# Expert passes with twelve resident up slabs instead of eight, and PE's up loop as three turns of twelve and eight behind them

## The chip, the cores and the metric

The kernel runs as one program on one core of a Trainium2 chip. The metric is the device time of one execution in microseconds. All data are float32. TensorE (PE) is fed by weight loads (PEld) that run beside its matmuls; VectorE (DVE) and ScalarE (ACT) empty the accumulators; SyncE (SP) issues all transfers from HBM, in program order, on one queue.

## What is computed

One step of a two-layer decoder for 288 tokens: 256 of a prompt and 8 sequences of 4 tokens. Each layer mixes tokens by three recurrent branches and then runs a SwiGLU. In layer 0 that is one dense SwiGLU, in layer 1 it is a mixture of eight experts, and only this last part is touched here:

```python
def swiglu(h, w1, w3, w2):
    return (jax.nn.silu(h @ w1) * (h @ w3)) @ w2

def moe_swiglu(h, router, w1, w3, w2):
    logits = (h @ router).astype(jnp.float32)
    top_v, top_i = lax.top_k(logits, TOP_K)          # TOP_K = 2 of 8
    probs = jax.nn.softmax(top_v, axis=-1)
    gate = jnp.sum(jax.nn.one_hot(top_i, N_EXPERTS, dtype=jnp.float32) * probs[..., None], axis=-2)
    out = jnp.zeros(h.shape, jnp.float32)
    for e in range(N_EXPERTS):
        out = out + gate[..., e:e + 1] * swiglu(h, w1[e], w3[e], w2[e]).astype(jnp.float32)
    return out.astype(h.dtype)
```

The model width is 1024 (KT = 8 tiles of 128), the hidden width 2816 (FT = 22 tiles of 128).

## The kernel before

**Passes.** The experts are worked off one after the other, one pass for each. A pass gathers the tokens of its expert into at most 88 columns (the four experts with the most tokens, `LARGE`) or 76 columns (the other three of the `FIXED` seven passes, and all `rest` passes behind them). In this profile there are eight passes: four of 88 columns, then four of 76, the last of which is the one turn of the `rest` loop.

**Slabs.** Weights come in slabs. An up slab is 128 x 1024 values, 512 KB, and gives one hidden tile of `h @ w1` (even numbers) or `h @ w3` (odd numbers); a pass has `UP_SLABS` = 44. A down slab belongs to `h @ w2`; a pass has 24, of which every third is 384 KB and the others 512 KB. For each slab PE makes 8 products, each as two halves of 64 rows (`narrow_products`, L447), so 16 matmuls. In float32 one matmul of the code is two MATMUL and two LDWEIGHTS records in the profile: 704 matmuls of an up part are 1408 records of each kind.

**Where slabs lie.** Up slab n lies in slot n % 8 of `ring` (`RING` = 8). Down slab d lies in slot d % 6 of `down_ring`, which is a part of `proj`. A semaphore for each slot (`slab_in`, `down_in`) tells PE that a slab has landed; one counter, `slab_done`, tells SP how many slabs PE has used up.

**PE's pass** (`expert`, L2679): a hardware loop `Fori` of five turns over eight up slabs (L2683), four up slabs behind it, the transposes of the scatter matrix (L2646), the gathering of the next pass's tokens (`gather_tokens`, L2617 and L2624), and a loop of four turns for the down part: two times three down slabs (L2659), two scattering products (L2670) and two transposes (L2677). The pass itself is the body of a hardware loop, and this body stands in PE's program three times: for the four large passes (L2717), for the three smaller ones (L2719), and for `rest` (L2722).

**SP's order in a pass** (L2526 to L2541, L2541 to L2555 for `rest`), which is what sets the order of the transfers: down slabs 0 to 5; up slabs 8 to 43; the first eight up slabs of the following expert, in the order `FREED` = 4, 5, 6, 7, 0, 1, 2, 3, each into the slot whose last slab of this pass is used up; down slabs 6 to 23. Each waits for its slot, and all behind it wait with it. The last pass too loads eight slabs of a following expert, though none follows. Up slab n waits until slab n - 8 is used up, down slab d until slab d - 6 is.

**Ahead of the passes.** While PE joins the branches of layer 1 (the pairs q of `join_slabs`; q below `BRANCH0` = 3 are the gates), SP loads the last two groups of `w_mix` slabs into the ring and then up slabs 0 to 7 of the first expert. `y_ret` (128 x 8 x 288) holds sums for the gates' products, `lora_w` (128 x 8 x 272) the weight sums of the first pair; neither is used after q = 2.

Of the kernel before, what the change touches and what calls it, by code (L numbers as in the profile page):

```python
# [22 lines left out]
D = 1024  # L23
# [7 lines left out]
KT = D // 128  # L31
# [7 lines left out]
FT = FF // 128  # L39
NE = 8  # L40
CAP, LAST_CAP, LARGE = 88, 76, 4
FIXED = NE - 1
# [8 lines left out]
RING = 8  # L51
# [34 lines left out]


UP_SLABS = 2 * FT
DOWN_SLABS = 24
HALF = T // 2  # L90
PAIRS_UP, PAIRS_DOWN = KT // 2, FT // 2
# [127 lines left out]
def build(nc, xT_in, w_mix, w_lora, w_rank, w_gkup, vec_in, vecf_in, router_in, w_ff, s_ret, s_gla, s_rw,  # L219
# [130 lines left out]
            self.end = w.at  # L350

    slab_in = [nc.alloc_semaphore(name=f"slab_in{s}") for s in range(RING)]
    slab_done = nc.alloc_semaphore(name="slab_done")
    rank_in = [nc.alloc_semaphore(name=f"rank_in{s}") for s in range(2)]
    wr = lora_w[:, :, :].rearrange("p k n -> p (k n)")[:, 0:512].rearrange("p (s n) -> p s n", s=2)
# [77 lines left out]
    def slab_arrived(pe, p, g, s):  # L433
        pe.wait_ge(slab_in[s], (g + (fills_before(layer, s) + fills(p, s) + 1)) * 16)

    def load_ff_slab(sp, e, j, s, done, n=KT):

        sp.wait_ge(slab_done, done)
        sp.dma_start(ring[:, s, 0:n], w_ff[e, j, :, 0:n]).then_inc(slab_in[s], 16)
# [5 lines left out]
            mm = nc.tensor.matmul(out, ring[:, s, k, :], x, start=(k0 + k == 0), stop=(k0 + k == last - 1))  # L445
        mm.then_inc(slab_done, 1)

    def narrow_products(pe, s, out, rhs, n=KT, k0=0, last=KT):

        for k in range(n):  # L450
            for c in range(2):
                mm = nc.tensor.matmul(out[64 * c:64 * c + 64], ring[:, s, k, 64 * c:64 * c + 64], rhs[:, k0 + k, :],  # L452
                                      start=(k0 + k == 0), stop=(k0 + k == last - 1))
        mm.then_inc(slab_done, 1)

    FIRST, MIDDLE, LAST_TWO = bank[0:6:3], bank[1:6:3], bank[2:6:3]
# [1665 lines left out]
    def mix_out(nc, block, sig, layer, delta, joined):  # L2122
# [31 lines left out]
        @block.sync  # L2154
        def _(sp):
            load_group(sp, S_RW_OUT, 1)
            load_first_group(sp, S_OUT)
            if dense:
                for j in range(FF_SLABS):
                    load_ff_slab(sp, 0, j, j % RING, FF0 + j - RING + 1, dense_slab_width(j))  # L2160
                    if j == UP_SLABS:
                        sp.wait_ge(sig("normed"), KT)
                        sp.dma_start(vec[:, :], vec_in[layer + 1]).then_inc(sig("next_vec"), 16)
                        sp.dma_start(lora_w[:, :, :], w_lora[layer + 1]).then_inc(sig("next_low"), 16)
                        sp.dma_start(gkup[:, :], w_gkup[layer + 1]).then_inc(sig("next_up"), 16)
                load_next_layer(sp)
                sp.wait_ge(sig("next_up"), 16)
            else:
                for j in range(RING):
                    load_ff_slab(sp, 1, j, j, FF0 + j - RING + 1)  # L2170
# [287 lines left out]
    def experts(nc, block, sig, layer, merge, rs):  # L2458
# [28 lines left out]
        HG, SC, DOWN, SUM = bank[4:8], bank[1], bank[2:4], bank[0]  # L2487
        OTOK, ADD = (bank[6], bank[4]), (bank[7], bank[5])
        FF0 = slabs_before(layer, len(STREAM))
        FREED = 4, 5, 6, 7, 0, 1, 2, 3  # L2490
        TILES = ((0, 128), (128, 128), (256, 32))

        def passes(eng):
# [12 lines left out]
        @block.sync  # L2506
        def _(sp):
            def freed_up(p, n):

                if n >= RING:  # L2510
                    return count(p, FF_SLABS, FF0 + n - RING + 1)
                return count(p, FF_SLABS, FF0 - FF_SLABS + max(range(n, UP_SLABS, RING)) + 1)

            def load_up(p, e, n):
                load_ff_slab(sp, e, n, n % RING, freed_up(p, n))

            def load_down(p, e, d):
                if d >= DRING:
                    sp.wait_ge(slab_done, count(p, FF_SLABS, FF0 + UP_SLABS + d - DRING + 1))
                else:  # L2520
                    sp.wait_ge(slab_done, count(p, FF_SLABS, FF0 - DRING + d + 1))
                n = slab_width(UP_SLABS + d)
                sp.dma_start(down_ring[:, d % DRING, 0:n], w_ff[e, UP_SLABS + d, :, 0:n]).then_inc(down_in[d % DRING], 16)

            e = 1
            for q in range(FIXED):  # L2526
                p = 0, q
                for d in range(DRING):
                    load_down(p, e, d)
                for n in range(RING, UP_SLABS):  # L2530
                    load_up(p, e, n)
                if q == 0:
                    sp.wait_ge(sig("ctl"), 1)
                following = sp.value_load(ctl[0:1, q:q + 1], min_val=1, max_val=NE)
                for n in FREED:
                    load_up((0, q + 1), following, n)
                for d in range(DRING, DOWN_SLABS):
                    load_down(p, e, d)
                e = following
            rest = passes(sp)  # L2540
            with sp.Fori(0, rest) as i:  # L2541
                e = sp.value_load(ctl[0:1, bass.ds(i + (FIXED - 1), 1)], min_val=1, max_val=NE)
                following = sp.value_load(ctl[0:1, bass.ds(i + FIXED, 1)], min_val=1, max_val=NE)
                p = i, FIXED
                for d in range(DRING):
                    load_down(p, e, d)
                for n in range(RING, UP_SLABS):
                    load_up(p, e, n)
                for n in FREED:
                    sp.wait_ge(slab_done, freed_up((i, FIXED + 1), n))  # L2550
                    settle(sp)
                    sp.dma_start(ring[:, n], w_ff[following, n]).then_inc(slab_in[n], 16)
                for d in range(DRING, DOWN_SLABS):
                    load_down(p, e, d)
            for k in range(0, KT, 2):  # L2555
                sp.wait_ge(sig("normed"), k + 2)
                sp.dma_start(yT_out[:, k:k + 2, :], hT[:, k:k + 2, :]).then_inc(sig("stored"), 16)
            sp.wait_ge(sig("stored"), 4 * 16)
            for s in range(RING):
                per = len(range(s, UP_SLABS, RING))  # L2560
                fill = fills_before(layer, s) + fills(len(STREAM), s) + FIXED * per + 1
                sp.wait_ge(slab_in[s], rest * (per * 16) + fill * 16)
                settle(sp)

        @block.tensor
        def _(pe):
# [62 lines left out]
            def up(p, cap, n, turn):  # L2629

                i, done = p
                s = n % RING
                per = len(range(s, UP_SLABS, RING))
                fill = fills_before(layer, s) + fills(len(STREAM), s) + done * per + n // RING + 1
                pe.wait_ge(slab_in[s], turn * 16 + (i * (per * 16) + fill * 16))
                pe.wait_ge(sig("w3_free" if n % 2 else "w1_free"), turn * (RING // 2) + count(p, FT, n // 2 + 1))
                if n in (2, 3):
                    pe.wait_ge(sig("oT"), count(p, KT, n - 1))
                narrow_products(pe, s, bank[n % 4][:, 0:cap], hg[:, :, 0:cap])

            def scatter_matrix(p):

# [36 lines left out]
            def expert(p, cap, next_cap):  # L2679

                pe.wait_ge(sig("hg"), count(p, 1, 1))
                settle(pe)
                with pe.Fori(0, UP_SLABS // RING) as g:  # L2683
                    for n in range(RING):
                        up(p, cap, n, g)
                for n in range(UP_SLABS // RING * RING, UP_SLABS):
                    up(p, cap, n, 0)
                scatter_matrix(p)
                pe.wait_ge(sig("otok"), count(p, KT, 2))
# [621 lines left out]
```

## Time and profile before

| | us |
|---|---|
| median of 3 runs | 2503.94 |
| lowest and highest | 2503.2, 2506.28 |
| the profiled execution, whole | 2506.55 |
| its span, first to last instruction | 2504.8 |
| outside the span | 1.75 |
| stretch of the eight expert passes in the span | 1772.0 to 2490.4 |

A row of the timeline shows instructions of one line of the code that follow each other without a wait; the time in brackets is how long the engine was idle before them, and what ended that. "issue" stands for a wait that nothing in the profile explains: no semaphore, no transfer of data. In the rows of the windows the share of the DMA engines goes slightly over 1 where packets overlap. Queue q1 carries the data, q8 and q14 carry instructions to the engines.

### The profile page before, as it was taken

Reading aid. Unit: us, or ns where it says so; the run is one execution under the profiler, and the core shown is the slowest. Engines: PE = TensorE matmul, PEld = TensorE weight load, DVE = VectorE, ACT = ScalarE, POOL = GpSimd, SP = SyncE. Lnnn points to the kernel's source line nnn. Section 1 sums busy time; section 2 is a strip of 40 time slices with the busy share of each in tenths; the row PEclk is TensorE's granted clock in tenths of the full one; section 3 lists DMA queues with packets and bytes.
Section 4 is the critical chain, followed back from the end, with each engine's and each line's share of the span. In section 5 each row is a group of like instructions: output and inputs, shape, how many; then the busy total and the mean of one; then the engine's idle time right before and its main releaser. Section 6 shows DMA issues by size and latency. Waiting matters only on the chain. (4 is left out here: it accounts for less than half of the span.)

```text
span 2504.8 us, 103575 instructions
## 1 busy us (share of the span) xinstructions
PE 2448.9 (98%) x45930; PEld 2047.9 (82%) x45930; DVE 1288.9 (51%) x3327; ACT 609.0 (24%) x1798; POOL 0.2 (0%) x4
## 2 busy tenths in 40 slices
PE   9999999999999999999999999999999999999998
PEld 8987666666698999898766666679899999888986
DVE  7666666666686676756665666667311111111111
ACT  2233333433311100223333334321111111111111
POOL 0000000000000000000000000000000000000000
PEclk9999999999999999999999999999999999999999
DMA  6334432222243444333443222234899999999997
GB/s 249 111 136 162 150 134 88 83 83 79 90 163 121 159 173 134 133 116 137 154 161 125 84 77 83 83 105 152 321 357 391 385 364 386 393 388 397 407 391 284
DMA packets 146066, 500.42 MB, mean 200 GB/s; under 512 B 18785, under 2 KB 23521, under 8 KB 143361
## 3 DMA queue, kind: packets, MB, share of 16 engines
q1 hardware_dynamic: 145792, 496.44, 54.3%
q8 instruction: 213, 3.49, 0.6%
q14 instruction: 61, 0.49, 0.1%
HBM read 476.08 MB, written 20.29 MB: 198 GB/s over the span
## 5 line engine op out<-in xcount | busy, mean ns | idle before, releaser
L299 PE MATMUL psum<-hT,ring 128*64 128x144 f32 (+1 forms) x4568 | 457.1, 345 | 3.8 <-DVE hT L2419 1.7
L452 PE MATMUL psum<-work,ring 128*64 128x88 f32 (+1 forms) x11264 | 423.8, 235 | 10.3 <-issue 4.3
L452 PEld LDWEIGHTS psum<-work,ring 128*64 128x64 f32 x11264 | 411.6, 136 | 23.4 <-issue 20.5
L299 PEld LDWEIGHTS psum<-hT,ring 128*64 128x64 f32 x4568 | 291.7, 137 | 97.6 <-issue 12.2
L2959 DVE TENSOR_TENSOR work<-psum,work 128x88 f32<-128x88 f32 x176 | 43.9, 249 | 363.5 <-PE psum L452 363.3
L2659 PE MATMUL psum<-work,proj 128*64 128x88 f32 (+1 forms) x5632 | 212.1, 234 | 4.1 <-issue 2.7
L2659 PEld LDWEIGHTS psum<-work,proj 128*64 128x64 f32 x5632 | 205.1, 136 | 10.8 <-issue 9.6
L1765 ACT ACTIVATE work<-psum 128x256 f32<-128x256 f32 (+4 forms) x320 | 104.0, 362 | 349.7 <-PE psum L1676 84.8
L299 PE MATMUL psum<-y_ret,work 128*64 128x144 f32 x2400 | 157.9, 288 | 0.8 <-DVE y_ret L529 0.8
L299 PE MATMUL psum<-work 128*64 128x144 f32 (+4 forms) x2096 | 154.1, 282 | 4.3 <-DVE work L1256 3.6
L299 PEld LDWEIGHTS psum<-y_ret,work 128*64 128x64 f32 x2400 | 150.3, 138 | 1.2 <-issue 1.2
L299 PEld LDWEIGHTS psum<-work 128*64 128x64 f32 (+2 forms) x2096 | 121.3, 136 | 30.7 <-issue 11.3
L2950 DVE TENSOR_TENSOR xT<-xT,psum 128x288 f32<-128x288 f32 x64 | 29.1, 454 | 224.9 <-PE psum L2670 223.9
L2744 ACT ACTIVATE work<-psum 128x88 f32<-128x88 f32 x176 | 43.0, 244 | 376.5 <-PE psum L452 376.3
L299 PE MATMUL psum<-y_ret,ring 128*64 128x144 f32 (+1 forms) x1280 | 126.8, 332 | 2.5 <-ACT work L1765 2.5
L299 PEld LDWEIGHTS psum<-y_ret,ring 128*64 128x64 f32 x1280 | 79.5, 137 | 18.4 <-ACT work L1765 4.5
L321 PE MATMUL psum<-hT,ring 128*128 128x288 f32 x252 | 72.8, 408 | 0.0
L1561 PEld LDWEIGHTS psum<-work 64*64 64x64 f32 x1408 | 47.3, 134 | 29.4 <-issue 17.7
L544 DVE TENSOR_TENSOR y_gla<-psum,y_gla 128x288 f32<-128x288 f32 x72 | 32.9, 458 | 73.3 <-PE psum L299 72.7
L2748 ACT ACTIVATE work<-psum 128x88 f32<-128x88 f32 x64 | 15.7, 245 | 222.8 <-PE psum L2659 222.8
L299 PE MATMUL psum<-hT,work 128*64 128x144 f32 x928 | 68.8, 287 | 0.0
L516 DVE TENSOR_TENSOR work<-ring 128x512 f32<-128x512 f32 (+1 forms) x90 | 54.6, 607 | 19.1 <-PE psum L299 19.1
(514 smaller groups left out, 3725.9 us busy)
## 6 DMA issues: line engine op xcount, KB each, us to landing
ring<-w_ff_dram SPq DMA_DIRECT2D x424, 512.0 KB, 6.9
ring<-w_mix_dram SPq DMA_DIRECT2D x256, 512.0 KB, 4.4
proj<-w_ff_dram SPq DMA_DIRECT2D x128, 512.0 KB, 5.5
proj<-w_ff_dram SPq DMA_DIRECT2D x64, 384.0 KB, 5.7
work<-s_gla_dram SPq DMA_DIRECT2D x8, 1024.0 KB, 5.4
gla_s_out<-work SPq DMA_DIRECT2D x8, 1024.0 KB, 4.7
work<-s_ret_dram SPq DMA_DIRECT2D x8, 512.0 KB, 5.6
ret_s_out<-work SPq DMA_DIRECT2D x8, 512.0 KB, 3.0
```

Of the source, the lines that this page charges most:

```text
L299: last = nc.tensor.matmul(out[64 * c:64 * c + 64], weights[:, 64 * c:64 * c + 64], x, start=start, stop=stop)
L321: mm = (in_halves if self.narrow else nc.tensor.matmul)(out, ring[:, s, k, :], rhs[:, k, :], start=(k == 0), stop=(k == KT - 1))
L452: mm = nc.tensor.matmul(out[64 * c:64 * c + 64], ring[:, s, k, 64 * c:64 * c + 64], rhs[:, k0 + k, :], start=(k0 + k == 0), stop=(k0 + k = ...
L516: op.tensor_tensor(s1, a21, a22, ALU.add).then_inc(sig("wsum"), 1)
L544: nc.vector.tensor_tensor(c[:, 1:3, :], two(LAST_TWO[side]), c[:, 5:7, :], ALU.add).then_inc(sig("outer"), 1)
L1561: last = mm(unit(half(W, r), c), half(AT, 1 - r)[:, c], half(X, 1 - r)[:, c], start=True, stop=True)
L1765: return nc.scalar.activation(out, in_, func, **kw)
L2659: last = mm(DOWN[m][64 * h:64 * h + 64, 0:cap], down_ring[:, d, k, 64 * h:64 * h + 64], hid[:, KT * c + k, 0:cap], start=(KT * c + k == 0) ...
L2744: ac(act1[:, f % 2, :], bank[2 * f % 4][:, 0:CAP], ACT.Silu).then_inc(sig("w1_free"), 1)
L2748: ac(oT[:, m % 2, :], DOWN[m % 2][:, 0:CAP], cp).then_inc(sig("oT"), 1)
L2950: tt(xT[:, k, :], xT[:, k, :], ADD[m % 2][:, 0:T], ALU.add).then_inc(sig("added"), 1)
L2959: tt(hid[:, f, :], bank[(2 * f + 1) % 4][:, 0:CAP], act1[:, f % 2, :], ALU.mult).then_inc(sig("w3_free"), 1)
```

## The change

- The up slabs get a ring of twelve slots, `UP_RING` = 12: the eight of `ring`, two in `y_ret` and two in `lora_w`, with a semaphore each (`extra_in`). Up slab n lies in slot n % 12. `down_ring` stays at six.
- PE's up loop has three turns of twelve slabs, and eight slabs stand behind it, in each of the three copies of the pass.
- SP loads up slabs 8 to 11 of the first expert while the branches are joined, as soon as the slabs of pair q = 2 are used up. In a pass it loads down slabs 0 to 5, up slabs 12 to 43, then twelve up slabs of the following expert, `FREED` = 8, 9, 10, 11, 0, ..., 7, then down slabs 6 to 23. Up slab n waits until slab n - 12 is used up.
- `narrow_products` is written with `in_halves`; the matmuls are the same, and the profile names them by another line (L300 of the changed file in place of L452).

```diff
+UP_RING = 12
...
+    extra_in = [nc.alloc_semaphore(name=f"extra_in{s}") for s in range(UP_RING - RING)]
+    up_in = slab_in + extra_in
...
+    extra_slots = [x.rearrange("p k n -> p (k n)")[:, D * j:D * j + D].rearrange("p (k n) -> p k n", k=KT)
+                   for x in (y_ret[:, :, :], lora_w[:, :, :]) for j in range(2)]
+    up_slots = [ring[:, s] for s in range(RING)] + extra_slots
...
             load_group(sp, S_RW_OUT, 1)
+            if not dense:
+                sp.wait_ge(slab_done, join_done(BRANCH0 - 1))
+                for n in range(RING, UP_RING):
+                    sp.dma_start(up_slots[n], w_ff[1, n]).then_inc(up_in[n], 16)
             load_first_group(sp, S_OUT)
...
-        FREED = 4, 5, 6, 7, 0, 1, 2, 3
+        FREED = 8, 9, 10, 11, 0, 1, 2, 3, 4, 5, 6, 7
...
-                if n >= RING:
-                    return count(p, FF_SLABS, FF0 + n - RING + 1)
-                return count(p, FF_SLABS, FF0 - FF_SLABS + max(range(n, UP_SLABS, RING)) + 1)
+                if n >= UP_RING:
+                    return count(p, FF_SLABS, FF0 + n - UP_RING + 1)
+                return count(p, FF_SLABS, FF0 - FF_SLABS + max(range(n, UP_SLABS, UP_RING)) + 1)
...
-                for n in range(RING, UP_SLABS):
+                for n in range(UP_RING, UP_SLABS):
                     load_up(p, e, n)
...
-                with pe.Fori(0, UP_SLABS // RING) as g:
-                    for n in range(RING):
+                with pe.Fori(0, UP_SLABS // UP_RING) as g:
+                    for n in range(UP_RING):
                         up(p, cap, n, g)
-                for n in range(UP_SLABS // RING * RING, UP_SLABS):
+                for n in range(UP_SLABS // UP_RING * UP_RING, UP_SLABS):
                     up(p, cap, n, 0)
```

PE's program in the first copy of the pass, before: the end of the loop's turn (slabs 6 and 7), the loop's branch, the four slabs behind it and the scatter transposes.

```order
L2635 ISA
L2636 ISA
L452 MATMUL psum<-work,ring 64x88 x32
L2683 REGISTER_ALU
L2683 COMPARE_AND_BRANCH
L2635 ISA
L2636 ISA
L452 MATMUL psum<-work,ring 64x88 x32
L2636 REGISTER_ALU
L452 MATMUL psum<-work,ring 64x88 x32
L2644 REGISTER_ALU
L2646 MATMUL psum<-table,work 88x128 x2
```

The same place now, from slabs 8 and 9 of the turn (in `y_ret`) on.

```order
L300 MATMUL psum<-work,y_ret 64x88 x32
L2649 ISA
L300 MATMUL psum<-work,lora_w 64x88 x32
L2696 REGISTER_ALU
L2696 COMPARE_AND_BRANCH
L2648 ISA
L2649 ISA
L300 MATMUL psum<-work,ring 64x88 x32
L2649 REGISTER_ALU
L300 MATMUL psum<-work,ring 64x88 x32
L2648 REGISTER_ALU
L2649 REGISTER_ALU
```

The loop's body grew from 128 to 192 matmuls and the part behind it from 64 to 128, so a copy of the pass has 128 matmuls more.

SP's program around the transfers for the following expert, first pass, before: the end of the up slabs, the reading of the expert's number, the first two of the eight.

```order
L439 DMA ring<-w_ff_dram 128x1024 x36
L2534 TENSOR_LOAD ctl
L2534 ISA x2
L439 ISA
L439 DMA ring<-w_ff_dram 128x1024
```

The same place now, with the first four of the twelve and the fifth.

```order
L2529 DMA ring<-w_ff_dram 128x1024 x8
L2548 TENSOR_LOAD ctl
L2548 ISA x2
L2529 ISA
L2529 DMA y_ret<-w_ff_dram 128x1024
L2529 ISA
L2529 DMA y_ret<-w_ff_dram 128x1024
L2529 ISA
L2529 DMA lora_w<-w_ff_dram 128x1024
L2529 ISA
L2529 DMA lora_w<-w_ff_dram 128x1024
```

Between the last up slab of a pass and its down slab 6 there stand twelve transfers now, eight before; ahead of them in the pass there are 32 up slabs to load instead of 36.

## Rows read from the trace of the kernel before

**Rows 1.** The page: span, engines, the queues of section 3.

```profile
span 2504.8 us, 103575 instructions
...
PE 2448.9 (98%) x45930; PEld 2047.9 (82%) x45930; DVE 1288.9 (51%) x3327; ACT 609.0 (24%) x1798; POOL 0.2 (0%) x4
...
q8 instruction: 213, 3.49, 0.6%
```

**Rows 2.** The chain that ended last, the passes: start us, us, what.

```profile
1864.59 54.50 PE psum L452 x1408
1919.09 0.51 PE psum L2646 x3
...
1955.88 54.54 PE psum L452 x1408
...
2226.38 10.93 PE psum L452 x320
```

**Rows 3.** The timeline of PEld, sixth pass: start us, us, what, [idle before <-releaser].

```profile
2226.37 18.28 PEld L452 LDWEIGHTS psum<-work,ring 128*64 128x64 f32 x544 [0.58 <-issue]
2244.94 1.12 PEld L452 LDWEIGHTS psum<-work,ring 128*64 128x64 f32 x32 [0.28 <-DMA ring<-w_ff_dram]
2246.43 2.28 PEld L452 LDWEIGHTS psum<-work,ring 128*64 128x64 f32 x64 [0.37 <-issue]
...
2279.43 0.17 PEld L2646 LDWEIGHTS psum<-table,work 128*88 128x88 f32 x2
...
2289.92 3.01 PEld L2659 LDWEIGHTS psum<-work,proj 128*64 128x64 f32 x88 [0.19 <-DMA proj<-w_ff_dram]
2293.34 3.14 PEld L2659 LDWEIGHTS psum<-work,proj 128*64 128x64 f32 x88 [0.40 <-issue]
...
2313.31 19.46 PEld L452 LDWEIGHTS psum<-work,ring 128*64 128x64 f32 x576 [0.55 <-issue]
```

**Rows 4.** Windows, whole core: one large pass, then ten-us pieces of the sixth.

```profile
1864.00:1955.00 91.00, 90.70 (x2235) 87.12 (x2234) 13.29 (x41) 11.95 (x41) 0.00 (x0) 1.00 0.99 379
...
2250.00:2260.00 10.00, 9.52 (x256) 8.78 (x253) 1.00 (x4) 0.98 (x4) 0.00 (x0) 1.00 1.03 410
...
2290.00:2300.00 10.00, 9.72 (x250) 8.70 (x252) 1.04 (x3) 1.34 (x7) 0.00 (x0) 1.00 1.03 407
2300.00:2310.00 10.00, 9.85 (x260) 8.84 (x256) 0.91 (x2) 1.17 (x5) 0.00 (x0) 1.00 0.97 363
2310.00:2320.00 10.00, 9.71 (x264) 8.81 (x262) 1.41 (x4) 2.70 (x7) 0.00 (x0) 1.00 0.99 363
```

**Rows 5.** DMA of 1900 to 2100, queues: packets, MB, share of 16 engines.

```profile
q1 hardware_dynamic: 21531, 76.30, 99.9%
q14 instruction: 4, 0.03, 0.1%
```

**Rows 6.** DMA of 1866 to 1867, and of 2145 to 2146.

```profile
q8 instruction: 1, 0.02, 5.8%
...
q8 instruction: 1, 0.02, 6.3%
```

**Rows 7.** The timeline of PEld, first time through the second copy (pass five).

```profile
2138.28 8.12 PEld L452 LDWEIGHTS psum<-work,ring 128*64 128x64 f32 x243 [0.49 <-issue]
2147.54 0.53 PEld L452 LDWEIGHTS psum<-work,ring 128*64 128x64 f32 x13 [1.14 <-issue]
...
2194.84 0.86 PEld L2659 LDWEIGHTS psum<-work,proj 128*64 128x64 f32 x24
2196.54 4.29 PEld L2659 LDWEIGHTS psum<-work,proj 128*64 128x64 f32 x127 [0.83 <-issue]
2201.25 0.86 PEld L2659 LDWEIGHTS psum<-work,proj 128*64 128x64 f32 x24 [0.42 <-issue]
```

**Rows 8.** The timeline of SP while the branches are joined, before the passes.

```profile
1703.18 21.38 SPq L420 DMA_DIRECT2D ring<-w_mix_dram  x8
1732.92 22.85 SPq L439 DMA_DIRECT2D ring<-w_ff_dram  x8
```

More of the change, by code:

```diff
@@ L434, in slab_arrived, with up_fills @@
         pe.wait_ge(slab_in[s], (g + (fills_before(layer, s) + fills(p, s) + 1)) * 16)
+    extra_slots = [x.rearrange("p k n -> p (k n)")[:, D * j:D * j + D].rearrange("p (k n) -> p k n", k=KT)
+                   for x in (y_ret[:, :, :], lora_w[:, :, :]) for j in range(2)]
+    up_slots = [ring[:, s] for s in range(RING)] + extra_slots
+    def up_fills(s):
+        return fills_before(layer, s) + fills(len(STREAM), s) if s < RING else 0
     def load_ff_slab(sp, e, j, s, done, n=KT):
@@ L446, in slab_products, with narrow_products @@
         mm.then_inc(slab_done, 1)
[L448 to L453, printed above, removed]
+    def narrow_products(out, slab, rhs):
+        for k in range(KT):
+            mm = in_halves(out, slab[:, k, :], rhs[:, k, :], k == 0, k == KT - 1)
         mm.then_inc(slab_done, 1)
@@ L2508, in freed_up @@
             def freed_up(p, n):
-                if n >= RING:
-                    return count(p, FF_SLABS, FF0 + n - RING + 1)
-                return count(p, FF_SLABS, FF0 - FF_SLABS + max(range(n, UP_SLABS, RING)) + 1)
+                if n >= UP_RING:
+                    return count(p, FF_SLABS, FF0 + n - UP_RING + 1)
+                return count(p, FF_SLABS, FF0 - FF_SLABS + max(range(n, UP_SLABS, UP_RING)) + 1)
             def load_up(p, e, n):
-                load_ff_slab(sp, e, n, n % RING, freed_up(p, n))
+                sp.wait_ge(slab_done, freed_up(p, n))
+                sp.dma_start(up_slots[n % UP_RING], w_ff[e, n]).then_inc(up_in[n % UP_RING], 16)
             def load_down(p, e, d):
@@ L2546, in _ @@
                     load_down(p, e, d)
-                for n in range(RING, UP_SLABS):
+                for n in range(UP_RING, UP_SLABS):
                     load_up(p, e, n)
@@ L2551, in _ @@
                     settle(sp)
-                    sp.dma_start(ring[:, n], w_ff[following, n]).then_inc(slab_in[n], 16)
+                    sp.dma_start(up_slots[n], w_ff[following, n]).then_inc(up_in[n], 16)
                 for d in range(DRING, DOWN_SLABS):
@@ L2558, in _ @@
             sp.wait_ge(sig("stored"), 4 * 16)
[L2559 to L2562, printed above, removed]
+            for s in range(UP_RING):
+                per = len(range(s, UP_SLABS, UP_RING))
+                sp.wait_ge(up_in[s], rest * (per * 16) + (up_fills(s) + FIXED * per + 1) * 16)
                 settle(sp)
@@ L2631, in up @@
                 i, done = p
[L2632 to L2636, printed above, removed]
+                s = n % UP_RING
+                per = len(range(s, UP_SLABS, UP_RING))
+                fill = up_fills(s) + done * per + n // UP_RING + 1
+                pe.wait_ge(up_in[s], turn * 16 + (i * (per * 16) + fill * 16))
+                pe.wait_ge(sig("w3_free" if n % 2 else "w1_free"), turn * (UP_RING // 2) + count(p, FT, n // 2 + 1))
                 if n in (2, 3):
                     pe.wait_ge(sig("oT"), count(p, KT, n - 1))
-                narrow_products(pe, s, bank[n % 4][:, 0:cap], hg[:, :, 0:cap])
+                narrow_products(bank[n % 4][:, 0:cap], up_slots[s], hg[:, :, 0:cap])
             def scatter_matrix(p):
```

## The prediction

> **What bounds the kernel now.** I read the page first: PE is busy for 98% of a span of 2504.8 us [rows 1]. That says that PE is nearly always occupied, not that it is the limit, so next come the chain that ended last and PE's timeline for the expert passes, the only part that the change touches in earnest. They show two regimes.
>
> In a pass of 88 columns the up part is one piece of 1408 records in 54.5 us without a wait [rows 2], 1.24 us a slab. One pass after the other takes 91.3 us (1864.59 to 1955.88). Here PE is the limit.
>
> In a pass of 76 columns PE needs 1.09 us a slab (320 records, ten slabs, in 10.93 us [rows 2]). It keeps that up for 17 slabs, then waits for a transfer, and from there on stops before every pair of slabs for 0.2 to 0.4 us [rows 3]: 13 pairs from 2246.43 to 2279.43, 2.54 us a pair, where PE alone would need 2.19. In that stretch the DMA engines move 410 GB/s [rows 4], which is 1.28 us for 512 KB, 2.56 for a pair. So the small passes go at the speed of the transfers. Were no slab late, the up part would take 44 x 1.09 = 48.0 us instead of 53.1 (2226.37 to 2279.43): 5.1 us of waiting in each of four passes, 20 us in all. That is what the twelve slots are aimed at.
>
> **The change part by part.**
>
> *Slabs 8 to 11 of the first expert, loaded early.* Four more transfers of 512 KB, 5.1 us of DMA time, are queued at q = 2. The next transfers behind them on SP's queue start at 1703.18 in this profile and the last eight end at 1755.8 [rows 8], eight transfers spread over 21 us in each group because they wait for slots, so the four fit between. Cost 0; without the cover at most 5.
>
> *Twelve slots in the up part.* A pass moves 60 slabs of 512 KB and 8 of 384 KB, 34.6 MB, before and after: 84.4 us at 410 GB/s, against 86.9 us for the sixth pass (2226.37 to 2313.31 [rows 3]). Nothing is taken away, so a ring can gain only what the DMA engines do not use: 2.5 us there. The question is where PE waits instead. SP's queue is in order, so I count what stands in it ahead of down slab 6 at the start of a pass: before, the last four or so of down slabs 0 to 5, 36 up slabs, 8 of the following expert, and slab 6 itself, 49 transfers; now 4 + 32 + 12 + 1 = 49. Down slab 6 is the 49th either way and lands at the same moment. Before, PE starts it at 2289.92 after a short wait for its transfer, and waits again 3.4 us later [rows 3]: it comes just in time, 10.5 us behind the end of the up part. Now PE ends the up part 5.1 us earlier and waits about 5 us more for down slab 6. Saved 4 x 5.1, paid back 4 x 5.1. The same holds in the last pass, where twelve slabs that nobody uses, not eight, stand ahead of it.
>
> What is left is the 2.5 us a pass of unused transfer time. It lies where PE uses down slabs slowly and SP waits for slots: 407 GB/s until 2300, then 363 [rows 4]. Those waits are on down slabs 12 to 23 and on the first up slab of the next pass, which have the slots they had. So 0, with a gain of 4 x 2.5 = 10 us as the bound and 2 us of loss as the other. In the large passes the DMA engines move 379 GB/s on average [rows 4] and nothing is late now: 0.
>
> *PE's program.* This is the part that I think decides. Of its 44 slabs a copy of the pass writes out 20 instead of 12. A matmul of the code is four instructions for the engine, as the records show (1408 MATMUL and as many LDWEIGHTS for 704). Counted through the program, a copy has 329 matmuls and 44 other instructions, 1360 in all; now 457 and 55, 1883. The whole program of PE has 55,232, and q8 brought 213 packets of 16.4 KB [rows 1]: one packet is about 256 instructions, and each part of the program came once. The trace confirms the size. On the first way through the second copy PE stops with "issue", and two such stops lie 127 weight loads and as many matmuls apart, 254 instructions [rows 7]: it stops where a new packet begins. From the first of them (243 weight loads in) the second copy begins some 15 instructions behind a border, and the first copy, 5.3 packets earlier, three quarters into a packet.
>
> So before, the first copy touches seven packets, the last by a few instructions. As PE enters that one, at the end of the first pass of this copy, another is brought ahead: the packet at 1866 [rows 6]. Eight, then, and from 1900 to 2100, over two further jumps back to the start of the copy, q8 brings nothing at all [rows 5]. The engine holds at least eight packets, and the trace shows no code of more than eight that runs twice. Now the first copy is 7.4 packets from three quarters into one: it touches nine, with one ahead ten. The second touches eight, with one ahead nine. If the store is the round eight that the trace shows full, the packet that the jump back needs has been overwritten each time.
>
> The Trainium skill, "Runtime: NRT & Kernel Launch", section "Instruction fetch mechanics", gives PE 128 KiB for instructions, 2048 of them, filled as a FIFO in blocks of 16 KiB, and says that a branch to a target not held has to wait for its fetch. The packets agree (16.4 KB), and by that rule both looping copies outgrow the store. The same section also speaks of a window of two pages; a copy of 5.3 packets that loops with no fetch [rows 5] speaks against that for PE.
>
> The price of a fetch: in pass five PE enters the packet before the stop after 3.7 slabs, at 2142.3; the next one is being moved at 2145 [rows 6] and PE goes on at 2147.54 [rows 7]: 5.2 us. The packet at 1866 is moved 2.6 us after the pass ended (1863.8), the same first half. At a jump back:
> - First copy: the first packet is wholly exposed, 5.2, of which 0.5 lie in a wait that PE has there anyway [rows 3]. Only a quarter of that packet is left, 1.1 us of work, so the second is exposed by 4.0. Further borders, if their packets are fetched again too, cost about 0.3 each, as 256 instructions are 4.8 us of work at 88 columns. Sum 9.3 us, on PE's path. Three jumps: 28 us.
> - Second copy: 5.2 - 0.5, and then a whole packet of work covers most of the next fetch. PE has 5 us of slack in a small pass, but SP's next transfer waits for PE's first slab, so the DMA engines run dry for most of this time. I take 4 us. Two jumps: 8 us.
> - The third copy runs once; its stops are as before.
>
> **Sum**: 0 + 0 + 28 + 8 = 36 us on the profiled span of 2504.8: 2541, and with 1.75 us outside 2542.5. The profiled run is 2.6 us over the median of 2503.94, so 2503.94 + 36 = **2540 us**. The price of a jump has no row of its own. Bounds: only half a fetch, 2.5 us, is exposed at each of five jumps, 12 us; or all are whole and every border of every refetched copy stops PE, 3 x 11 + 2 x 10 = 53 us. So 2516 to 2557 for this case.
>
> **Rivals.**
> - *The store holds the loop* (more than eight packets, or what is fetched ahead does not push out the start). Then the sum is 0 within 2 us: 2502 to 2507, no change. For it: the trace shows no limit, only that eight fit. Against: it would have to be nine at least, ten for the first copy. Chance 0.18.
> - *The ring does gain*, on the other side: the waits of the up part go and down slab 6 is not as late as I count, since with twelve slots the DMA engines never run dry at a pass's end. Worth up to 10 us by unused transfer time, 2494, and 2484 if all 20 us of waiting went. It decides if the transfers that PE finds waiting at the start of the down part are fewer than 13. Against it: the count of 49, and the wait at 2289.92. It also needs the store to hold. Chance 0.11.
> - *The jump back misses* as above: 0.71.
>
> **How the numbers follow.** The likeliest case gives 2540. Its own range, 2516 to 2557, leaves out a little of its 0.71. To hold 8 in 10 the range must take in the case of no change: **2500 to 2558**. A difference under 0.2%, 5 us, is about what a measurement of this kernel cannot tell from none. Faster 0.11, same 0.18, slower 0.71.
>
> **What the profile of after would show.** If right: q8 with clearly more than 219 packets (213 and six for the longer program), some of them near the start of passes two, three, four, six and seven; idle time "issue" of 4 to 9 us before the first up slab of these passes and of the large ones again after some 16 matmuls; up parts of 76 columns of about 48 us and then a wait of about 5 us on a down slab at the second turn. If the count of 49 is wrong, that last wait is missing and a small pass is shorter than 86 us. If q8 shows 219 packets, the store holds the loop and my main term is nothing.

## The result: 2.2% slower, for the reason that was forecast and by more than was forecast

| | before | after |
|---|---|---|
| median, us | 2505.11 (4 runs) | 2558.79 (4 runs) |
| lowest and highest | 2503.2, 2506.68 | 2557.12, 2564.22 |
| span of the profiled execution | 2504.8 | 2555.4 |
| packets on q8 (instructions) | 213 | 267 |

The ratio is 1.0217, with a 95% interval of 1.0202 to 1.0233. The change costs 53.7 us. The prediction was 2540, with 2500 to 2558 as its range, so the time lies 0.8 us above the range, and two of the four runs (2557.12 and 2557.22) lie inside it: the direction and the mechanism were right, the price was not.

The page of the changed kernel, the lines that answer to [rows 1]:

```profile
span 2555.4 us, 103524 instructions
...
PE 2447.3 (96%) x45930; PEld 2054.4 (80%) x45930; DVE 1290.3 (50%) x3327; ACT 609.0 (24%) x1798; POOL 0.2 (0%) x4
...
q8 instruction: 267, 4.37, 0.7%
```

PE's busy time is the same as before (2447 against 2449 us), the span is 50.6 us longer, and q8 brought 54 packets more. Six of them are the longer program; 48 came more than once. The timeline of PEld shows where they are waited for, first at the start of the second pass (start us, us, what, [idle before <-releaser]):

```profile
1863.67 0.17 PEld L2690 LDWEIGHTS psum<-table,work 128*88 128x88 f32 x2 [0.44 <-issue]
1869.86 2.05 PEld L300 LDWEIGHTS psum<-work,ring 128*64 128x64 f32 x27 [6.02 <-issue]
1872.35 9.29 PEld L300 LDWEIGHTS psum<-work,ring 128*64 128x64 f32 x228 [0.44 <-issue]
...
1926.38 0.16 PEld L2659 LDWEIGHTS psum<-table,work 128*88 128x88 f32 x2
...
2258.90 0.16 PEld L2690 LDWEIGHTS psum<-table,work 128*88 128x88 f32 x2 [0.44 <-issue]
2265.56 10.32 PEld L300 LDWEIGHTS psum<-work,ring 128*64 128x64 f32 x256 [6.50 <-issue]
...
2281.46 0.80 PEld L300 LDWEIGHTS psum<-work,lora_w 128*64 128x64 f32 x21 [2.02 <-issue]
...
2316.61 0.99 PEld L300 LDWEIGHTS psum<-work,ring 128*64 128x64 f32 x28 [1.22 <-issue]
```

Before, a pass started after 0.55 us [rows 3]. Now passes 2, 3, 4, 6 and 7 start after 6.0, 6.8, 7.4, 6.5 and 6.3 us of "issue": the five jumps back, and no others. Pass 5, the first time through the second copy, starts after 0.55 us, and pass 8, the first through the third, after 1.41 (1.39 before).

There is a second thing in these rows that the prediction did not have. The first 27 weight loads after the stop take 2.05 us, 76 ns each, where 38.5 ns is the pace of a large pass. The windows of those stretches say why (us, PE, PEld, DVE, ACT and POOL busy (records), PEclk, DMA share, GB/s):

```profile
1866.00:1869.80 3.80, 0.00 (x0) 0.00 (x0) 0.00 (x0) 0.00 (x0) 0.00 (x0) 0.58 0.46 182
...
1869.80:1872.30 2.50, 2.31 (x26) 2.05 (x27) 0.00 (x0) 0.00 (x0) 0.00 (x0) 0.50 0.03 7
...
2265.50:2270.00 4.50, 4.43 (x80) 4.44 (x82) 0.06 (x1) 0.24 (x1) 0.00 (x0) 0.57 0.20 56
```

The granted clock fell to 0.50, 1.2 GHz instead of 2.4, while PE stood still, and stayed there for some time after PE went on; behind the jump into the sixth pass it is 0.57 over 4.5 us (last row). And the DMA engines moved 7 and 56 GB/s: SP waits for PE's first slab, so the stop of PE became a stop of the transfers.

Pass by pass, from the first weight load of one to that of the next, in us:

| pass | before: up part, rest | after: up part, rest | longer |
|---|---|---|---|
| 1 | 54.3, 38.2 | 54.6, 44.6 | 6.6 |
| 2 | 54.4, 36.8 | 56.5, 45.6 | 10.9 |
| 3 | 54.5, 36.8 | 57.0, 46.0 | 11.7 |
| 4 | 54.4, 36.8 | 56.6, 39.1 | 4.5 |
| 5 | 53.3, 34.8 | 51.9, 43.0 | 6.8 |
| 6 | 53.1, 33.9 | 52.1, 42.7 | 7.9 |
| 7 | 52.8, 34.6 | 52.9, 38.2 | 3.7 |
| 8 and the end | 104.0 in all | 103.9 in all | -0.1 |

The stop at a jump is counted in the "rest" of the pass ahead of it. The large passes lose 33.7 us (366.3 to 400.0), the small ones with the end 18.3, and the expert passes begin 1.4 us earlier.

One forecast sign is missing in this profile. The up parts of passes 5 to 7 take 51.9, 52.1 and 52.9 us, not 48, and PE does not wait for down slab 6 at the second turn. The stops for instructions stand in the place of that wait. That wait shows only in kernels without these stops, below.

### The profile page after: what moved, and what is told of

It is laid out like the page before. It is cut to its first block and busy times, and to the rows that moved or that the text cites. A ratio compares the mean times of both kernels' runs of the same rounds, so it can differ in the third digit from the quotient of the medians.

```text
span 2555.4 us, 103524 instructions
## 1 busy us (share of the span) xinstructions
PE 2447.3 (96%) x45930; PEld 2054.4 (80%) x45930; DVE 1290.3 (50%) x3327; ACT 609.0 (24%) x1798; POOL 0.2 (0%) x4
## 3 DMA queue, kind: packets, MB, share of 16 engines
q1 hardware_dynamic: 146368, 498.54, 53.3%
## 5 line engine op out<-in xcount | busy, mean ns | idle before, releaser
L300 PE MATMUL psum<-hT,ring 128*64 128x144 f32 (+1 forms) x4568 | 457.5, 346 | 4.3 <-DVE hT L2432 1.7
L300 PE MATMUL psum<-work,ring 128*64 128x88 f32 (+2 forms) x8800 | 360.6, 241 | 40.4 <-issue 40.1
L300 PEld LDWEIGHTS psum<-work,ring 128*64 128x64 f32 x8800 | 344.9, 138 | 45.3 <-issue 44.9
L300 PEld LDWEIGHTS psum<-hT,ring 128*64 128x64 f32 x4568 | 292.9, 137 | 97.4 <-issue 12.7
L1774 ACT ACTIVATE work<-psum 128x256 f32<-128x256 f32 (+4 forms) x320 | 104.0, 362 | 349.8 <-PE psum L1685 84.8
L300 PE MATMUL psum<-work 128*64 128x144 f32 (+4 forms) x2096 | 154.8, 282 | 4.3 <-DVE work L1265 3.6
L300 PE MATMUL psum<-y_ret,work 128*64 128x144 f32 x2400 | 156.2, 286 | 0.7 <-DVE y_ret L538 0.7
L300 PEld LDWEIGHTS psum<-y_ret,work 128*64 128x64 f32 x2400 | 148.6, 137 | 1.1 <-issue 1.1
L300 PEld LDWEIGHTS psum<-work 128*64 128x64 f32 (+2 forms) x2096 | 122.0, 136 | 30.6 <-issue 11.3
L300 PE MATMUL psum<-y_ret,ring 128*64 128x144 f32 (+1 forms) x1280 | 127.2, 332 | 2.5 <-ACT work L1774 2.5
L300 PEld LDWEIGHTS psum<-y_ret,ring 128*64 128x64 f32 x1280 | 79.9, 137 | 18.4 <-ACT work L1774 4.5
L300 PE MATMUL psum<-hT,work 128*64 128x144 f32 x928 | 69.1, 287 | 0.0
L300 PE MATMUL psum<-work,lora_w 128*64 128x88 f32 (+1 forms) x1536 | 60.7, 234 | 7.7 <-issue 7.7
```

The lines of the kernel that those rows point to most:

```text
L300: last = nc.tensor.matmul(out[64 * c:64 * c + 64], weights[:, 64 * c:64 * c + 64], x, start=start, stop=stop)
L1774: return nc.scalar.activation(out, in_, func, **kw)
```

## The experiments

Two theories were set against each other. **The store**: PE holds eight packets of instructions; a looping copy of the pass that needs more than eight, with the one fetched ahead, finds its start gone at each jump back. **The ring**: the twelve slots, their places in `y_ret` and `lora_w`, or the order of the transfers cost the time.

### The code alone

```diff
 # the kernel before
-                with pe.Fori(0, UP_SLABS // RING) as g:
+                with pe.Fori(0, 4) as g:
                     for n in range(RING):
                         up(p, cap, n, g)
-                for n in range(UP_SLABS // RING * RING, UP_SLABS):
+                for n in range(4 * RING, UP_SLABS):
                     up(p, cap, n, 0)
```

> The kernel before with its ring of eight and its order of transfers, only PE's up loop has four turns of eight slabs and twelve behind it instead of five turns and four. A copy of the pass is then 1883 instructions, as in the changed kernel, against 1360. If the store for PE's instructions is what costs (eight packets of 256): five jumps back miss, about 50 us over before, 2550 to 2560, with idle times of 6 to 7 us at the starts of passes 2, 3, 4, 6 and 7 and about 48 packets more on q8 than the program is longer. If the ring, its slots in y_ret and lora_w or the order of the transfers is what costs, this kernel stays at 2505 within 3 us.

Measured: 2580.48 us, ratio 1.0307 (1.0290 to 1.0324), 75 us slower than before, 267 packets on q8, the same number as in the changed kernel. The stops stand at the same five jumps:

```profile
1872.74 2.05 PEld L452 LDWEIGHTS psum<-work,ring 128*64 128x64 f32 x27 [6.70 <-issue]
...
1976.77 2.05 PEld L452 LDWEIGHTS psum<-work,ring 128*64 128x64 f32 x27 [7.14 <-issue]
```

The store is confirmed: no slot, address or order of a transfer differs from the kernel before. But both theories had this kernel at 2560 at most. It is 22 us slower than the changed kernel, so with the long program the ring of twelve is worth 22 us. Its up parts take 59.2, 58.3 and 58.4 us in passes 2 to 4 against 56.5, 57.0 and 56.6 with twelve slots, and 57.5 and 58.1 against 52.1 and 52.9 in passes 6 and 7. Part of this difference is only a shift: in this kernel a stop of 1.25 to 1.54 us for a packet falls into the up parts of passes 2 to 4, where in the changed kernel it comes just behind them. Whole passes compare better. Of the 20 us between the two spans (2575.6 and 2555.4), 13.2 lie in passes 5 to 7, 3.3 in passes 1 to 4. In the small passes PE again waits before every pair of slabs, as in these rows of the sixth pass; in the changed kernel's there is no such wait:

```profile
2303.71 2.28 PEld L452 LDWEIGHTS psum<-work,ring 128*64 128x64 f32 x64 [0.28 <-issue]
2306.35 2.28 PEld L452 LDWEIGHTS psum<-work,ring 128*64 128x64 f32 x64 [0.36 <-issue]
```

With eight slabs in hand PE uses up the ring while the transfers are still making good the stop.

### The ring alone

```diff
 # the changed kernel
-                with pe.Fori(0, UP_SLABS // UP_RING) as g:
-                    for n in range(UP_RING):
+                with pe.Fori(0, 4) as g:
+                    for n in range(8):
                         up(p, cap, n, g)
-                for n in range(UP_SLABS // UP_RING * UP_RING, UP_SLABS):
-                    up(p, cap, n, 0)
+                    with pe.If(g < 3):
+                        for n in range(8, UP_RING):
+                            up(p, cap, n, g)
```

> The changed kernel with its ring of twelve and its order of transfers, but PE's up loop has four turns, the last four slabs of the body skipped in the last turn, and nothing behind it: a copy is 1362 instructions, as before. If the store is the whole cost and down slab 6 is the 49th transfer either way: 2502 to 2508, no idle time over 1 us at the start of a pass, small passes whose up part takes 48 us and whose second down turn waits about 5 us. If the ring gains: 2485 to 2497, and the wait on down slab 6 is missing. If the ring itself costs: 2520 or more.

Measured: 2509.40 us, ratio 1.0020 (1.0010 to 1.0029), 213 packets; 1.4 us above the 2502 to 2508 that was expected. With the program as short as before, 49 of the 54 us are gone. This kernel also shows what the ring does when nothing hides it. The sixth pass, timeline of PEld, the end of its up part and its down part:

```profile
2226.56 8.54 PEld L300 LDWEIGHTS psum<-work,ring 128*64 128x64 f32 x256 [0.57 <-issue]
...
2274.68 0.17 PEld L2659 LDWEIGHTS psum<-table,work 128*88 128x88 f32 x2
...
2284.82 0.16 PEld L2690 LDWEIGHTS psum<-table,work 128*88 128x88 f32 x2 [0.44 <-issue]
2290.83 8.06 PEld L2672 LDWEIGHTS psum<-work,proj 128*64 128x64 f32 x176 [5.84 <-DMA proj<-w_ff_dram]
...
2300.30 5.89 PEld L2672 LDWEIGHTS psum<-work,proj 128*64 128x64 f32 x176 [0.18 <-issue]
```

The up part takes 48.1 us, 5 us less than before, and PE then waits 5.84 us for down slab 6: the 49th transfer is about where it was, 64.3 us behind the start of the pass against 63.6 [rows 3]. So the ring only moves the wait. It is not for nothing, though: the small passes take 91.4, 89.4 and 89.0 us (passes 5 to 7) against 88.1, 86.9 and 87.4. The row behind the long wait tells a large part of why: 176 loads in 8.06 us, where the next 176 take 5.89. Thirteen stops of 0.2 to 0.4 us left the clock alone; one of 5.84 halved it, which cost 2.2 us more. In passes 5 and 7 the waits are 3.46 and 5.14 us, and the 176 loads behind them take 8.73 and 8.23 us. So the half clock costs 2.9, 2.2 and 2.3 us, about what these passes lose (3.3, 2.4 and 1.6). The granted clock behind the wait of 5.84 us:

```profile
2290.80:2294.00 3.20, 3.17 (x50) 3.17 (x52) 0.00 (x0) 0.00 (x0) 0.00 (x0) 0.50 0.97 383
```

### A size in between, and where the borders lie

Three turns of sixteen slabs on the ring of eight, the last four skipped in the last turn, make a copy of 1622 instructions.

```diff
 # the kernel before; the counts that a slab waits for follow the turn of sixteen
-                pe.wait_ge(slab_in[s], turn * 16 + (i * (per * 16) + fill * 16))
+                pe.wait_ge(slab_in[s], turn * 32 + (i * (per * 16) + fill * 16))
...
-                with pe.Fori(0, UP_SLABS // RING) as g:
-                    for n in range(RING):
+                with pe.Fori(0, 3) as g:
+                    for n in range(12):
                         up(p, cap, n, g)
-                for n in range(UP_SLABS // RING * RING, UP_SLABS):
-                    up(p, cap, n, 0)
+                    with pe.If(g < 2):
+                        for n in range(12, 16):
+                            up(p, cap, n, g)
```

> The kernel before with its ring of eight, PE's up loop with three turns of sixteen slabs, the last four skipped in the last turn: a copy is 1622 instructions, 6.3 packets. By the count of borders the first copy touches eight packets and one is fetched ahead, nine; the second touches seven, with one ahead eight. If the store holds exactly eight and the one ahead counts: passes 2, 3 and 4 start with 6 to 7 us of idle time, passes 6 and 7 do not; about 33 us over before, 2538. If it holds fewer: both copies miss, 2555. If it holds nine or ten: 2505.

Measured: 2531.93 us, ratio 1.0108 (1.0087 to 1.0128), 6 us under the 2538 that was expected. The starts of passes 2, 3 and 4, and then of 6 and 7:

```profile
1868.53 56.36 PEld L452 LDWEIGHTS psum<-work,ring 128*64 128x64 f32 x1408 [6.49 <-issue]
...
1968.47 55.88 PEld L452 LDWEIGHTS psum<-work,ring 128*64 128x64 f32 x1408 [7.04 <-issue]
...
2066.89 56.15 PEld L452 LDWEIGHTS psum<-work,ring 128*64 128x64 f32 x1408 [6.10 <-issue]
...
2249.29 18.17 PEld L452 LDWEIGHTS psum<-work,ring 128*64 128x64 f32 x544 [0.54 <-issue]
...
2336.88 3.24 PEld L452 LDWEIGHTS psum<-work,ring 128*64 128x64 f32 x96 [0.59 <-issue]
```

Two copies of the same length: the one that touches eight packets misses three times out of three, the one that touches seven never. If so, moving the first copy must cure it. 76 one-instruction steps ahead of the copies do that, increments of a semaphore for which nothing waits any more:

```diff
 # the kernel with sixteen slabs written out
             keep_busy(1, bank[3])
+            for _ in range(76):
+                pe.sem_inc(sig("shift"), 1)
             with pe.Fori(0, LARGE) as i:
```

> The kernel e3_ring8_16written (16 slabs written out, 1622 instructions a copy, 2532 us) with 76 increments of an unused semaphore ahead of the copies in PE's program. They move the first copy from three quarters into a packet to just behind a border, so that it touches seven packets instead of eight, like the second one. If the count of borders is what decides: no pass starts with more than 1 us of idle time, q8 has no packet that comes twice, and the time falls to 2505 to 2512, although the program is longer. If the size of a copy is what costs, or the skipped slabs: 2532 stays, or rises by the 4 us or so of the increments.

Measured: 2522.42 us, ratio 1.0070 (1.0052 to 1.0089). All jumps are cured, q8 shows 217 packets (213 before, whose program is 862 instructions or 3.4 packets shorter), and pass 2 starts like before:

```profile
1785.89 16.18 PEld L452 LDWEIGHTS psum<-work,ring 128*64 128x64 f32 x365 [11.45 <-issue]
...
1881.43 54.25 PEld L452 LDWEIGHTS psum<-work,ring 128*64 128x64 f32 x1408 [0.57 <-issue]
```

The expected 2505 to 2512 was missed by the price of the cure. I took the increments for 4 us; PE stood still for 11.45 us ahead of pass 1, where it was 0.79, and the up part of that pass then took 58.7 instead of 54.3, with the clock at 0.50 until 1790 and two stops of 0.92 and 1.32 us. Those 15 us taken off, 2507 remain.

### How much is fetched again

The changed kernel brings nine or ten packets at each jump, the one with sixteen slabs only two (222 packets in all). In the latter the eighth packet is entered by a few instructions only. The same with 40 increments instead of 76 ends the copy a quarter into it:

> The kernel e3_ring8_16written with 40 increments of an unused semaphore ahead of the copies instead of none. The first copy still touches eight packets, but it ends a quarter into the eighth instead of a few instructions into it. In e3_ring8_16written each jump brought only two packets again, in the changed kernel nine or ten. If that was because the last packet was barely entered: here each of the three jumps of the first copy brings nine packets, q8 has about 244 and the down parts of passes 2 to 4 get stops of about 1 us. If it is because eight packets are touched rather than nine: q8 has about 222 again. In both cases passes 2 to 4 start with 6 to 7 us of idle time and passes 6 and 7 do not. The increments themselves cost about 8 us once.

Measured in one run: 2548.17 us, where the kernel before took 2503.16 beside it; span 2546.3, and

```profile
q8 instruction: 244, 4.00, 0.6%
```

That is the 244 that stood for "barely entered": each jump of the first copy brings the whole copy again. Passes 2 to 4 start after 6.7, 6.6 and 6.5 us and stop again 7 loads later for 1.6 to 2.2 us, at the next border. The stops of about 1 us that were expected in the down parts are not there; stops of 0.7 to 1.2 us come in the up part instead, 383 loads in. And the changed kernel, its first copy moved so that it touches eight packets instead of nine:

> The changed kernel with 76 increments ahead of the copies: the first copy touches eight packets instead of nine, the second, which touched eight, still does. If any copy that touches eight or more by more than a few instructions is fetched whole again at each jump: q8 stays at about 268 and the jumps cost what they did, so the time is the changed kernel's plus 10 to 15 us for the increments. If nine touched is what costs the whole copy: q8 falls to about 245 and passes 2 to 4 lose the stops in the down part.

Measured in one run, beside the same 2503.16: 2568.97 us and 265 packets. That is 10 us over the changed kernel, and PE stands still 10.6 us longer ahead of pass 1. Passes 2 to 4 take 101.8, 101.1 and 96.1 us against 102.2, 103.0 and 95.7 in the changed kernel, so eight touched costs about as much as nine. One packet too many costs the whole copy, then, not one packet. How the store chooses what it drops, and why a barely entered packet is milder, these runs don't show.

### Naming the jump ahead of time

```diff
 # the changed kernel, for both looping copies
-            with pe.Fori(0, LARGE) as i:
+            with nc.Fori(0, LARGE, engines=[mybir.EngineType.PE], hint_back_edge=True) as i:
```

> The changed kernel, unaltered but for an instruction at the head of the two looping copies that names the jump back ahead of time, so that its target can be fetched while the pass still runs. If the idle time at the jump is the fetch of the target: it falls from 6 to 7 us to under 2, the half clock behind it goes too, and 2559 becomes 2515 to 2530, since the other packets of the copy are still fetched again with stops of about 1 us. If the jump's cost is something else: 2559 stays.

Measured: 2545.76 us, ratio 1.0163 (1.0142 to 1.0183), 247 packets: 13 us better than the changed kernel, not 30. In the first copy the stop at the jump is down to 0.8 to 0.9 us and the next packet, which nobody named, is waited for instead, 26 loads later:

```profile
1868.16 1.12 PEld L300 LDWEIGHTS psum<-work,ring 128*64 128x64 f32 x26 [0.88 <-issue]
1873.36 6.78 PEld L300 LDWEIGHTS psum<-work,ring 128*64 128x64 f32 x103 [4.08 <-issue]
...
2259.62 8.53 PEld L300 LDWEIGHTS psum<-work,ring 128*64 128x64 f32 x256 [0.66 <-issue]
2323.22 6.88 PEld L2672 LDWEIGHTS psum<-work,proj 128*64 128x64 f32 x162 [5.74 <-DMA proj<-w_ff_dram]
```

In the second copy, which begins just behind a border, the hint cures both jumps, and the wait for down slab 6 appears at once in the place of the stops. Most of the gain lies there: passes 5 to 7 take 267.1 us against 280.9, passes 1 to 4 take 395.7 against 400.0.

### Using what the ring holds

If down slab 6 is late because twelve slabs of the following expert stand ahead of it, four of them can stand behind the down slabs, where the transfers had time left.

```diff
 # the kernel with the ring alone; the same in the loop for the rest
-                for n in FREED:
+                for n in range(0, 8):
                     load_up((0, q + 1), following, n)
                 for d in range(DRING, DOWN_SLABS):
                     load_down(p, e, d)
+                for n in range(8, 12):
+                    load_up((0, q + 1), following, n)
```

> The kernel e2_ring12_12written (ring of twelve, small copies, 2509.4 us) with another order of the transfers: of the twelve slabs for the following expert, numbers 0 to 7 stay ahead of down slabs 6 to 23 and numbers 8 to 11 go behind them. Down slab 6 is then the 45th transfer of a small pass instead of the 49th. If that count sets the wait: the wait of 5 to 6 us at the second down turn falls to under 1.5, the half clock behind it goes, the up part stays at 48 to 50 us, and with four transfers in hand at the end of a pass the engines do not run dry there: 2493 to 2503. If the transfers have no time left at all: the wait moves back into the up part and the time is 2505 to 2510.

Measured: 2497.99 us (2495.03 to 2500.93, 7 runs), ratio 0.9970 (0.9959 to 0.9982): 11 us faster than with the ring alone and 7.6 us faster than the kernel before. The sixth pass takes 85.8 us. Its second down turn, and windows of its down part and of the whole pass:

```profile
2287.12 3.02 PEld L2678 LDWEIGHTS psum<-work,proj 128*64 128x64 f32 x88 [0.19 <-DMA proj<-w_ff_dram]
2290.54 3.14 PEld L2678 LDWEIGHTS psum<-work,proj 128*64 128x64 f32 x88 [0.41 <-issue]
```

```profile
2224.70:2310.60 85.90, 83.86 (x2237) 77.51 (x2237) 13.54 (x41) 11.99 (x42) 0.00 (x0) 1.00 1.03 407
...
2300.00:2310.00 10.00, 10.00 (x246) 8.51 (x242) 1.43 (x4) 1.17 (x5) 0.00 (x0) 1.00 1.02 392
```

The transfers run at 407 GB/s over the whole pass; before it was 399, with a fall to 363 at its end [rows 4]. Passes 5 to 7 take 85.9, 85.8 and 86.9 us against 88.1, 86.9 and 87.4, and the last with the end 101.5 against 104.0. The up part takes 51.9 us, not the 48 to 50 that I expected: with the engines never dry, what is left of the waits is the bandwidth. The same idea on the ring of eight, which leaves four slabs ahead and not eight:

```diff
 # the kernel before; the same in the loop for the rest
-                for n in FREED:
+                for n in range(0, 4):
                     load_up((0, q + 1), following, n)
                 for d in range(DRING, DOWN_SLABS):
                     load_down(p, e, d)
+                for n in range(4, 8):
+                    load_up((0, q + 1), following, n)
```

> The kernel before (ring of eight, its PE program untouched) with the same idea: slabs 0 to 3 of the following expert ahead of down slabs 6 to 23, slabs 4 to 7 behind them. It tells the order apart from the ring. If the unused transfer time at the end of a pass is worth 2 us a small pass by the order alone: 2496 to 2501. If the ring of twelve is needed for it: 2503 to 2507. If four slabs in hand are too few to bridge PE's last up slabs: slower than 2507.

Measured: 2520.07 us, ratio 1.0062 (1.0048 to 1.0075). With only eight slots, up slab 8 now stands behind ten other transfers on the queue, four up slabs and six down slabs, and PE stops for it after eight slabs. In the sixth pass:

```profile
2232.23 8.53 PEld L452 LDWEIGHTS psum<-work,ring 128*64 128x64 f32 x256 [0.54 <-issue]
2243.16 12.50 PEld L452 LDWEIGHTS psum<-work,ring 128*64 128x64 f32 x320 [2.40 <-issue]
```

Even the large passes 2 to 4, which had no wait, lose 1.6 to 1.7 us each. So it is the twelve slots and the order together that gain; neither did alone in these kernels.

## Why the prediction failed in size

- **What bounds the kernel**: right. The small passes are held by the transfers, 5.1 us of waits in an up part; with them gone it takes 48.1 and 47.9 us (ring alone), 48.0 was computed.
- **The early load of four slabs, cost 0**: right within the scatter of the start of the passes. In the profiles with the early load and nothing added ahead of the copies they start between 1769.4 and 1773.5 us, in those without it between 1769.9 and 1772.4.
- **The ring, cost 0**: the count of 49 was right and with the short program the wait came where and about as long as forecast (3.5, 5.8 and 5.1 us in passes 5 to 7). The step that failed in it was "saved 4 x 5.1, paid back 4 x 5.1", which takes thirteen short waits and one long one for the same. The ring alone costs 4.0 us against the runs of the kernel before made beside it, 1.0020 with its interval above 1; the bound given, 2 us of loss, was too small. The long wait lowers the clock, 2.2 us in the sixth pass. In the changed kernel itself the long wait does not appear.
- **Which copies miss**: right. Nine and eight packets touched, five jumps, none at the first way through; and the five kernels whose length or place was changed for it miss and hold as the count of borders says.
- **The price of a jump, first copy, 9.3 us**: the terms were wrong, partly against each other. The stop for the target was put at 5.2 - 0.5 and is 6.0 to 7.4 less 0.55, so 18.6 us for three instead of 14. The stop for the second packet was put at 4.0 and is 0.35 to 0.63: the second is already under way when PE goes on (q8 moves a packet between 1869 and 1870, and PE goes on at 1869.86). The further borders stand in the sum with 0.6 a pass, two of 0.3, though nine packets have seven of them; behind the up parts of passes 2 to 4 they cost 2.3 to 2.6 us, mostly two stops of about 1 us. And the half clock behind each stop had no term at all; with the stop for the second packet the up parts of passes 2 to 4 are 2.1 to 2.5 us longer. Three jumps with all this: 33.7 us against 28 forecast.
- **The price of a jump, second copy, 4 us**: this is the step that failed worst. I took it that only the dry time of the transfers counts, since PE has 5 us of slack in a small pass. The stop itself is 6.0 and 5.8 us over the usual 0.55, and the slack is not there for it: the transfers stand still in the same microseconds. At 367 GB/s in the sixth pass (399 before) a pass takes 94.8 us. Nor did a packet of work cover most of the next fetch: in the sixth pass PE stops at three further borders, for 2.02, 1.22 and 1.97 us, and behind the last of them the clock falls to half again (last rows below). All small passes with the end lost 18.3 us against 8.

```profile
2265.60:2360.40 94.80, 83.94 (x2237) 79.46 (x2237) 13.54 (x41) 11.96 (x41) 0.00 (x0) 0.95 0.95 367
...
2323.39 7.28 PEld L2672 LDWEIGHTS psum<-work,proj 128*64 128x64 f32 x163 [1.97 <-issue]
...
2321.40:2323.40 2.00, 0.14 (x6) 0.03 (x3) 0.00 (x0) 0.00 (x0) 0.00 (x0) 1.00 1.02 410
2323.40:2327.40 4.00, 4.00 (x73) 4.00 (x73) 0.00 (x0) 0.00 (x0) 0.00 (x0) 0.57 1.04 411
```

- **What took the time out of the range**: 18.8 us lie between 2540 and 2558.79. The second copy has 10.3 of them and the first 5.7; the earlier start of the passes takes off 1.4, and the remaining 4.2 come from how the profiled executions lie to the medians (50.6 us between the spans, 53.7 between the medians) and from the base, 2505.11 and not 2503.94. Neither copy's term alone would have left the range; both together did, by 0.8 us, less than the four runs of the changed kernel scatter.

- **The rivals**: the store does not hold nine. The ring does gain, though not by the rival's mechanism: 22 us when the program is too long. With the short program and in the order of the changed kernel it loses 4; with its slabs queued in another order it gains 11 on that, and 7.6 us on the kernel before.

The half clock is read from rows and was not varied by itself. Which share of the 18.3 us it has, and which the borders, stays open, since the stops also took the place of the 5.1 us of waits in each up part.

## What to carry to other kernels

A loop whose body is unrolled further has a price that no row of the old profile shows: count the body in instructions as the engine gets them (here four for a float32 matmul), find the borders of the packets from the stops on the first way through, and compare with the longest loop that runs without a packet on the instruction queue. Where it does not fit, skipping a part of the body in the last turn kept the same twelve slabs a turn at the old length. And with the short program the deeper ring gained only with an order of the transfers that puts the deeper part where the engines would stand idle; count the transfers ahead of the next thing that is needed.

## What the runs showed of the hardware

- These runs are all borne out if PE keeps eight packets of 256 instructions, the one fetched ahead among them. A loop over seven touched packets runs without a fetch; one over eight stops at each jump for 6.0 to 7.4 us and, if the eighth is entered by more than a few instructions, fetches its whole body again. The Trainium skill, "Runtime: NRT & Kernel Launch", section "Instruction fetch mechanics", gives 2048 instructions for PE in a FIFO. The traces agree on the size; that the oldest packet is always the one dropped they do not bear out, since the kernel with sixteen slabs brought only two packets again at a jump. The section's remark on a window of two pages does not hold for PE here, where 5.3 packets loop with no fetch [rows 5].
- The granted clock fell to 0.50 when PE stood still for 6 to 7 us at a jump, and for 3.46 to 5.84 us before a slab, and some 3 to 6 us of work behind it ran at half pace. A stop of 1.97 us in the changed kernel's sixth pass had the same behind it, one of 2.02 us in the up part of that pass left the clock at 1.00; what makes the difference these runs don't show. Waits of 0.2 to 0.4 us before every second slab left it at 1.00.
- 76 increments of a semaphore in PE's program held PE up by 10.7 us, 0.14 us each, and 40 by 5.0 us, 0.12 us each. Whether a fetch of instructions is in that, these runs don't show.
